# Two transformer blocks on one core: the SBUF addresses of the stage buffers moved, two of them with padded tiles

## The chip, the cores and the metric

The kernel runs on one core of one Trainium2 chip. The metric is the device time of one execution in microseconds (us); three executions give a median, and one more was profiled. The result must equal the reference's output for 256 tokens of width 1024 in float32.

## What is computed

Two blocks in sequence, over one batch of 256 tokens. The first is a SwiGLU FFN, a mixer of three attention branches, and a second SwiGLU FFN, with layer norms. The second is a mixer of a gated delta rule and a sparse attention, a GEGLU FFN with a convolution, and a gated embedding. Cut to what the change touches:

```
def swiglu(x, w_gate, w_up, w_down):
    return (jax.nn.silu(x @ w_gate) * (x @ w_up)) @ w_down          # D=1024, D_FF=2816
...
    x = layer_norm(alpha * x + 0.5 * swiglu(x, ...), ...)            # FFN 0
    x = layer_norm(alpha * x + hybrid_mixer(x, ...), ...)            # o_m, o_d, o_s -> branches -> w_out
    x = layer_norm(alpha * x + 0.5 * swiglu(x, ...), ...)            # FFN 1
...
    mixed = (g_a * (ya @ w_a2d[i]) + g_b * (yb @ w_b2d[i])) @ w_o[i]
    h = h + rmsnorm(mixed, norm_mix_post[i])
    f = rmsnorm(h, norm_ffn_pre[i]) @ w_up[i]
    f = causal_dwconv(f, conv_ffn[i]) + conv_ffn_b[i]
    f_gate, f_val = jnp.split(f, 2, axis=-1)
    f = (jax.nn.gelu(f_gate) * f_val) @ w_down[i]                    # FFN 2
```

## The kernel before

Every float32 product is made of three matmuls in a rounded type (fp32r): a value is split into a high part and a low part, and `mm3` (L585) adds high·high, the cross product and low·high in PSUM. Of every operand of such a product there are therefore two buffers, made by `pair` (`weights_high` and `weights_low`, `xT_high` and `xT_low`, and so on).

All weights come as one stream of 343 full chunks of 512 KB. SP loads a chunk into one of four slots of `ring`, ScalarE rounds it into `weights_high` (L1449), GpSimd subtracts to get `weights_low` (L536), and TensorE waits for that (`weights`, L563). A chunk is 8 blocks of 128x128. The semaphores `used`, `hi_ready` and `lo_ready` pass the slots round.

TensorE runs its program in one written order. A matmul has a stationary operand, loaded by a weight load (LDWEIGHTS, the row PEld of the profile) that runs beside the matmul before it, and a moving operand. Two forms occur:

- Feature-major: the stationary operand is a weight block of 128x128 and the moving one an activation tile of 256 columns. Of this form are the FFNs' gate and up, most projections, the branches (moving operand `oT`) and the delta rule's and sparse attention's output projections (`mix_part`, L1384, moving operand `yT`).
- Token-major: the stationary operand is 128 columns of an activation tile and the moving one up to 512 columns of weights. Of this form are the FFNs' down projections (`down`, stationary `hT`), the projections `w_out` and `w_o` (stationary `mT`), and some projections with `xT` as the stationary operand.

An FFN has 22 tiles of hidden features. After the first few, each step is one `gate_up` (48 matmuls of 256 columns) and one `down` (12 matmuls of 512 columns). VectorE makes the hidden tile `hf` and splits it into `hT_high` and `hT_low` (`split_hidden`, L2006), four tiles deep (GROUP). The delta rule's and attention's outputs are turned by TensorE, then split by ScalarE (`high_y`, L1858) and VectorE (`low_y`, L2594) into `yT`.

SBUF is laid out by the order of declarations in `build`. The tensors that live throughout come first: `ring`, `weights_high` and `weights_low` all begin at 128 modulo 1024 bytes of their partition (a block at 128 or 640), and `xT_high` and `xT_low` at 64, with tiles of 1024 bytes. After a filler of 144 words, `fill_stage`, comes one region that the stages use in turn: the FFNs (`hT`, `hf`, `act_buf`, `gel`), block one (`qkT`, `mT1`, `v1`, `oT` and others) and block two (`cv`, `mT2`, `yT`, `pE` and others). In the kernel before, this region begins at 32 modulo 1024 bytes, and so do all tiles of `hT`, `mT`, `oT` and `yT`, since each tile is 1024 bytes long.

Of the kernel before, what the change touches and what calls it, by code (L numbers as in the profile page):

```python
# [25 lines left out]
ALU = mybir.AluOpType  # L26
ACT = mybir.ActivationFunctionType
AX = mybir.AxisListType
F32 = mybir.dt.float32
F32R = mybir.dt.float32r  # L30

P = 128
T = 256
# [7 lines left out]
GROUP = 4  # L41
# [267 lines left out]
def build(nc, x_tm, x_fm, p_fm, stream, consts, cols, big_rows, small_rows, out, const_at):  # L309
# [4 lines left out]
    with ExitStack() as ctx:  # L314
        in_ffn, block_one, block_two, early = ExitStack(), ExitStack(), ExitStack(), ExitStack()

        def sb(name, shape, where=ctx, dtype=F32):
            return where.enter_context(nc.sbuf_tensor(name, [P] + list(shape), dtype))

        def pair(name, shape, where=ctx):  # L320

            return sb(name + "_high", shape, where, F32R), sb(name + "_low", shape, where, F32R)

        S = {n: ctx.enter_context(nc.semaphore(n)) for n in SEMS}
        arrived = [ctx.enter_context(nc.semaphore(f"arrived{i}")) for i in range(RING)]
        acc = ctx.enter_context(nc.psum_tensor("acc", [P, 4, 512], F32))
# [16 lines left out]
        nmx2 = sb("nmx2", [2, 4])  # L343
        den2 = sb("den2", [2, 4])
        coef2 = sb("coef2", [2, 4])
        sb("fill_stage", [144])
        hT = pair("hT", [GROUP, T], in_ffn)
        hf = sb("hf", [2, T], in_ffn)
        act_buf = sb("act_buf", [2, 2 * T], in_ffn)
        gel = sb("gel", [2, T], in_ffn)  # L350
# [43 lines left out]
        dec = sb("dec", [8, P], early)  # L394
        kv_tm = sb("kv_tm", [4, 512], early)
        early.close()
        yT = pair("yT", [8, T], block_two)
        sb("pad3", [3 * 8 * P + 4 * 512 - 16 * T], block_two)
        rcs = sb("rcs", [2, 16, 64], early, F32R)
        early.close()  # L400
        both_pT = sb("both_pT", [2, 2, 384], early)
# [156 lines left out]
        def _(pe):  # L558
# [4 lines left out]
            def weights(n):  # L563

                b = at[0]
                at[0] += n
                if b % CB == 0:
                    ch = b // CB
                    pe.wait_ge(S["lo_ready"], ch + 1)
                    release[0] = ch > 0  # L570
                return parts(b, n)
# [13 lines left out]
            def mm3(o, lhsT, rhs, start, stop, **kw):  # L585

                mm(o, lhsT[0], rhs[0], start, False, **kw)
                mm(o, lhsT[0], rhs[1], False, False, **kw)
                return mm(o, lhsT[1], rhs[0], False, stop, **kw)

            def cut(both, *at_):
                return tuple(x[(slice(None),) + at_] for x in both)
# [467 lines left out]
            for first in range(0, H1 + 4, 2):  # L1060
                for i in sb_heads(first):
                    o = take(f"sbz{i}")
                    r = 64 * (i % 2)
                    q, k = qkT[r:r + 64, 12 + i // 2, :], qkT[r:r + 64, 15 + i // 2, :]
# [4 lines left out]
                for h in sb_heads(first - 2):  # L1069
                    o = take(f"sbr{h}")  # L1070
# [10 lines left out]
                for h in sb_heads(first - 4):  # L1081
                    o = take(f"sbo{h}")
# [54 lines left out]
            for t in range(4):  # L1137
                o = take(f"l2_{t}")
# [71 lines left out]
            o = take("gcum")  # L1210
            pe.wait_ge(S["g_ready"], 1)
            for ch in range(2):
                last = nc.tensor.matmul(o[:, HG * ch:HG * ch + HG], c("upper"), gk[:, HG * ch:HG * ch + HG], start=True, stop=True)
            done(last)
            for ch in range(2):
                o = take(f"grow{ch}")
                pe.wait_ge(S["g_rows"], 1)
                for h in range(HG):
                    last = nc.tensor.matmul(o[:, h * P:(h + 1) * P], grow[:, HG * ch + h, :], c("upper"), start=True, stop=True)
# [3 lines left out]
            for ch in range(2):  # L1223
                assert jobs[now[0]][0] == f"brow{ch}"
                now[0] += 1
                for h in range(HG):
                    last = nc.tensor.matmul(acc[:, 2 + ch, h * P:(h + 1) * P], brep[:, HG * ch + h, :], ident, start=True, stop=True)
# [3 lines left out]
            for ch in range(2):  # L1231
                t0 = P * ch
                for name, first in ((f"ktm{ch}", 4), (f"vtm{ch}", 8)):
                    o = take(name)
                    for h in range(HG):
                        last = nc.tensor.transpose(o[:, h * P:(h + 1) * P], cv[:, first + h, t0:t0 + P], ident)
                    done(last)
                for name, first in ((f"kk{ch}", 4), (f"qk2_{ch}", 0)):
                    o = take(name)
# [139 lines left out]
            def mix_part(o, b):  # L1379

                for k in range(4):
                    if b == 0 and k % 2 == 0:
                        pe.wait_ge(S["yT_ready"], k // 2 + 1)
                    last = mm3(o[:, b * T:b * T + T], weights(1), cut(yT, 4 * b + k), k == 0, k == 3)  # L1384
                return last

            o = [bank(f"mix{n}") for n in range(3)]
# [16 lines left out]
            for n in range(3, 8):  # L1404
                o = take(f"mix{n}")
# [5 lines left out]
            for half in range(2):  # L1411
                w = [weights(4) for k in range(2)]
                for tok in range(2):
                    o = take(f"ple{2 * half + tok}")
# [12 lines left out]
        def _(act):  # L1427
# [430 lines left out]
            def high_y(k, order):  # L1858

                act.wait_ge(S["yT_turned"], order + 1)  # L1860
                nc.scalar.copy(yT[0][:, 2 * k:2 * k + 2, :].rearrange("p a t -> p (a t)"), acc[:, (k + 2) % 4, :]
                               ).then_inc(S["yT_high"], 1)

            def both_exp(e):
# [116 lines left out]
        def _(dve):  # L1981
# [24 lines left out]
            def split_hidden(n, f, it):  # L2006
                value = NF * n + f + 1 + GROUP * it
                dve.wait_ge(S["h_made"], value)
                v.tensor_copy(hT[0][:, f % GROUP, :], hf[:, f % 2, :]).then_inc(S["h_high"], 1)
                dve.wait_ge(S["h_high"], value)  # L2010
                v.tensor_tensor(hT[1][:, f % GROUP, :], hf[:, f % 2, :], hT[0][:, f % GROUP, :].bitcast(F32), ALU.subtract  # L2011
                                ).then_inc(S["hidden"], 1)

            def conv_col(i, it):
# [186 lines left out]
            def low(out, value, high):  # L2201

                return v.tensor_tensor(out, value, high.bitcast(F32), ALU.subtract)  # L2203
# [390 lines left out]
            def low_y(k, order):  # L2594

                dve.wait_ge(S["yT_high"], order + 1)
                hi, lo = (x[:, 2 * k:2 * k + 2, :].rearrange("p a t -> p (a t)") for x in yT)
                low(lo, acc[:, (k + 2) % 4, :], hi).then_inc(S["yT_ready"], 1)

            def both_bias(e):  # L2600

# [229 lines left out]
```

## Time and profile before

| | us |
|---|---|
| median of 3 runs | 1124.36 |
| lowest and highest | 1123.49, 1124.64 |
| the profiled execution | 1123.59 |
| its span, first to last instruction | 1121.8 |

| engine | busy us | share of the span | instructions |
|---|---|---|---|
| TensorE matmuls (PE) | 1094.6 | 98% | 8110 |
| TensorE weight loads (PEld) | 1023.9 | 91% | 8110 |
| GpSimd (POOL) | 902.6 | 80% | 695 |
| ScalarE (ACT) | 621.2 | 55% | 1002 |
| VectorE (DVE) | 498.7 | 44% | 904 |

Matmuls overlap: a matmul of 256 columns is shown as some 280 ns long, while the next one starts after some 115 ns. So the busy time of PE tells whether TensorE had work, not how fast it did it. How fast is read from the starts: the time from the first start to the last, divided by the number of matmuls between them, is called the interval below. The length that the profile shows for a matmul moves with it, by about as many ns.

### The profile page before, as it was taken

The numbers are of one execution on the slowest core, as the hardware profiler recorded it, in microseconds if no ns is written. First come the engines' busy times: TensorE is split into PE (matmuls) and PEld (weight loads), VectorE is DVE, ScalarE is ACT, GpSimd is POOL, SyncE is SP. The second block draws the span as 40 slices with busy tenths as digits, with TensorE's granted clock in tenths as the row PEclk, the third lists the DMA queues.
The fourth block names the chain that finished last, engine by engine and source line by source line (L and its number), as shares of the span: only waits on it lengthen the run. The fifth ranks groups of instructions, "written<-read, shape, count | busy, mean of one in ns | idle before, by whom it ended". The sixth has DMA issues, their size and how long they took to land.

```text
span 1121.8 us, 22284 instructions
## 1 busy us (share of the span) xinstructions
PE 1094.6 (98%) x8110; PEld 1023.9 (91%) x8110; DVE 498.7 (44%) x904; ACT 621.2 (55%) x1002; POOL 902.6 (80%) x695
## 2 busy tenths in 40 slices
PE   8999999999999999999999999999999999999997
PEld 7999998999998998999999899889999798999985
DVE  4422113202456554421126655774766256445563
ACT  4444444654667866544443775555666565555564
POOL 6999997897664596999999589577355898999985
PEclk9999999999999999999999999999999999999999
DMA  7866665676442364766665466335234565666662
GB/s 254 275 205 194 190 194 158 206 229 185 117 129 80 128 186 144 227 203 198 188 184 178 140 190 191 114 116 161 63 95 129 181 195 168 191 197 187 189 182 79
DMA packets 52774, 191.29 MB, mean 171 GB/s; under 512 B 5856, under 2 KB 6112, under 8 KB 52320
## 3 DMA queue, kind: packets, MB, share of 16 engines
q1 hardware_dynamic: 50688, 182.47, 53.1%
q10 hardware_dynamic: 2016, 7.81, 2.0%
q8 instruction: 53, 0.87, 0.3%
q14 instruction: 17, 0.14, 0.0%
HBM read 189.21 MB, written 1.05 MB: 170 GB/s over the span
## 4 chain that ended last, share of the span: by engine, by line
POOL 54%; issue 29%; PE 14%; POOLq 1%; ACT 1%; DMA 0%; DVE 0%; SPq 0%; DVEq 0%; ACTq 0%
POOL weights_low L536 54%; PE banks L578 8%; PE acc L578 6%; DMA ring<-in_stream 0%; POOLq L542 0%; POOLq L533 0%; ACT tmp L1697 0%; ACT tmp L1967 0%; ACT weights_high L1449 0%; DVE res L2173 0%; POOL stat L550 0%; DVE xs L2185 0%; POOLq L314 0%; PE banks L687 0%; SPq L497 0%
## 5 line engine op out<-in xcount | busy, mean ns | idle before, releaser
L536 POOL TENSOR_TENSOR weights_low<-ring,weights_high 128x512 fp32r<-128x512 f32 x686 | 899.5, 1344 | 207.6 <-ACT weights_high L1449 205.4
L1449 ACT CAST weights_high<-ring 128x1024 fp32r<-128x1024 f32 x343 | 356.0, 1047 | 215.7 <-PE banks L578 133.5
L578 PE MATMUL banks<-xT_high,weights_high 128*128 128x256 f32 x1264 | 351.6, 278 | 1.1 <-POOL weights_low L536 1.1
L578 PE MATMUL banks<-xT_low,weights_high 128*128 128x256 f32 x1264 | 350.5, 277 | 0.0
L578 PE MATMUL banks<-xT_high,weights_low 128*128 128x256 f32 x1264 | 350.4, 277 | 0.0
L578 PEld LDWEIGHTS banks<-xT_high,weights_high 128*128 128x128 f32 x1264 | 237.6, 188 | 4.1 <-issue 1.5
L578 PEld LDWEIGHTS banks<-xT_low,weights_high 128*128 128x128 f32 x1264 | 237.6, 188 | 2.3
L578 PEld LDWEIGHTS banks<-xT_high,weights_low 128*128 128x128 f32 x1264 | 237.9, 188 | 0.0
L2002 DVE TENSOR_TENSOR hf<-act_buf,banks 128x256 f32<-128x256 f32 x40 | 16.8, 421 | 225.7 <-ACT act_buf L1475 211.5
L578 PE MATMUL acc<-xT_high,weights_high 128*128 128x256 f32 x408 | 109.2, 287 | 1.9 <-ACT xT_high L1550 1.0
L578 PE MATMUL acc<-xT_high,weights_low 128*128 128x256 f32 x408 | 105.2, 278 | 0.0
L578 PE MATMUL acc<-weights_high,hT_high 128*128 128x512 f32 x264 | 104.1, 394 | 1.0 <-POOL weights_low L536 1.0
L578 PE MATMUL acc<-weights_low,hT_high 128*128 128x512 f32 x264 | 104.0, 394 | 0.0
L578 PE MATMUL acc<-weights_high,hT_low 128*128 128x512 f32 x264 | 103.3, 397 | 0.0
L578 PE MATMUL acc<-xT_low,weights_high 128*128 128x256 f32 x408 | 93.7, 278 | 0.6 <-DVE xT_low L2203 0.6
L578 PEld LDWEIGHTS acc<-xT_high,weights_high 128*128 128x128 f32 x408 | 75.2, 188 | 6.3 <-ACT xT_high L1550 1.7
L578 PEld LDWEIGHTS acc<-xT_high,weights_low 128*128 128x128 f32 x408 | 75.1, 188 | 0.0
L578 PEld LDWEIGHTS acc<-xT_low,weights_high 128*128 128x128 f32 x408 | 67.9, 188 | 0.8 <-DVE xT_low L2203 0.8
L2011 DVE TENSOR_TENSOR hT_low<-hf,hT_high 128x256 fp32r<-128x256 f32 x66 | 65.3, 990 | 2.3
L2027 DVE SCALAR_TENSOR_TENSOR act_buf<-banks,col,act_buf 128x255 f32<-128x255 f32 (+1 forms) x80 | 34.9, 478 | 58.7 <-ACT act_buf L1493 56.2
L578 PEld LDWEIGHTS acc<-weights_high,hT_low 128*128 128x128 f32 x264 | 49.6, 188 | 11.7
L578 PEld LDWEIGHTS acc<-weights_high,hT_high 128*128 128x128 f32 x264 | 49.6, 188 | 11.3 <-POOL weights_low L536 1.5
(362 smaller groups left out, 1579.4 us busy)
## 6 DMA issues: line engine op xcount, KB each, us to landing
ring<-in_stream SPq DMA_DIRECT2D x343, 512.0 KB, 3.7
rows<-in_big_rows ACTq DMA_DIRECT2D x3, 1024.0 KB, 7.6
rows<-in_big_rows ACTq DMA_DIRECT2D x3, 512.0 KB, 4.1
cst<-in_consts ACTq DMA_DIRECT2D x3, 470.5 KB, 6.5
xs<-in_x_tm ACTq DMA_DIRECT2D x2, 512.0 KB, 5.9
out<-xs SPq DMA_DIRECT2D x4, 256.0 KB, 2.1
gates<-in_x_fm SPq DMA_DIRECT2D x2, 256.0 KB, 4.1
ring<-in_stream SPq DMA_DIRECT2D x2, 256.0 KB, 4.1
```

The lines of the kernel that those rows point to most:

```text
L536: last = nc.gpsimd.tensor_tensor(wlo[:, slot, hs], ring[:, slot, hs], whi[:, slot, hs].bitcast(F32), ALU.subtract)
L578: ins = nc.tensor.matmul(o, lhsT, rhs, start=start, stop=stop, **kw)
L1449: nc.scalar.copy(whi[:, ch % RING, :], ring[:, ch % RING, :]).then_inc(S["hi_ready"], 1)
L2002: v.tensor_tensor(hf[:, f % 2, :], act_buf[:, f % 2, 0:T], ffn_tile(n, f, it)[:, T:2 * T], ALU.mult).then_inc(S["h_made"], 1)
L2011: v.tensor_tensor(hT[1][:, f % GROUP, :], hf[:, f % 2, :], hT[0][:, f % GROUP, :].bitcast(F32), ALU.subtract).then_inc(S["hidden"], 1)
L2027: last = v.scalar_tensor_tensor(buf, ffn_tile(2, f, it)[:, half * T:half * T + T - sh], conv_col(3 * (half * NF + f) + tap, it), buf, ALU. ...
```

## The change

The filler `fill_stage` grows from 144 to 152 words, so the region of the stages begins at 64 modulo 1024 bytes, 32 bytes later. The tiles of `hT` are declared 272 words long in place of 256 (1088 bytes apart) and those of `yT` 264 words long (1056 bytes apart); the 16 or 8 words behind the first 256 of each are never used. All instructions that touch `hT` and `yT` take the slice `0:T` of a tile, which turns two contiguous operands of `yT` (512 elements) into two runs of 256. A filler behind `yT` shrinks by as much.

| buffer | bytes modulo 1024 before | after |
|---|---|---|
| `weights_high`, `weights_low` (blocks) | 128, 640 | the same |
| `xT_high`, `xT_low` (all tiles) | 64 | the same |
| `hT_high`, tiles 0 to 3 | 32 each | 64, 128, 192, 256 |
| `hT_low`, tiles 0 to 3 | 32 each | 320, 384, 448, 512 |
| `yT_high`, tiles 0 to 7 | 32 each | 64, 96, 128 and so on to 288 |
| `yT_low`, tiles 0 to 7 | 32 each | 320, 352, 384 and so on to 544 |
| `mT1`, `mT2`, `oT`, `pE` (all tiles) | 32 | 64 |
| `hf`, `act_buf`, `gel` | 32 | 576 |

No instruction is added, removed or moved on any engine: the order of each engine's program is the same, and only these shapes differ (128x512 becomes 128x2x256 in the four casts at L1861 and the four subtractions of `low_y`).

```diff
@@ -343,8 +343,8 @@
-        sb("fill_stage", [144])
-        hT = pair("hT", [GROUP, T], in_ffn)
+        sb("fill_stage", [152])
+        hT = pair("hT", [GROUP, T + 16], in_ffn)
@@ -394,8 +394,8 @@
-        yT = pair("yT", [8, T], block_two)
-        sb("pad3", [3 * 8 * P + 4 * 512 - 16 * T], block_two)
+        yT = pair("yT", [8, T + 8], block_two)
+        sb("pad3", [3 * 8 * P + 4 * 512 - 16 * (T + 8)], block_two)
@@ -1381,7 +1381,7 @@
-                    last = mm3(o[:, b * T:b * T + T], weights(1), cut(yT, 4 * b + k), k == 0, k == 3)
+                    last = mm3(o[:, b * T:b * T + T], weights(1), cut(yT, 4 * b + k, slice(0, T)), k == 0, k == 3)
@@ -1858,7 +1858,7 @@
-                nc.scalar.copy(yT[0][:, 2 * k:2 * k + 2, :].rearrange("p a t -> p (a t)"), acc[:, (k + 2) % 4, :]
+                nc.scalar.copy(yT[0][:, 2 * k:2 * k + 2, 0:T], acc[:, (k + 2) % 4, :].rearrange("p (a t) -> p a t", a=2)
@@ -2006,9 +2006,9 @@
-                v.tensor_copy(hT[0][:, f % GROUP, :], hf[:, f % 2, :]).then_inc(S["h_high"], 1)
+                v.tensor_copy(hT[0][:, f % GROUP, 0:T], hf[:, f % 2, :]).then_inc(S["h_high"], 1)
...
-                v.tensor_tensor(hT[1][:, f % GROUP, :], hf[:, f % 2, :], hT[0][:, f % GROUP, :].bitcast(F32), ALU.subtract
+                v.tensor_tensor(hT[1][:, f % GROUP, 0:T], hf[:, f % 2, :], hT[0][:, f % GROUP, 0:T].bitcast(F32), ALU.subtract
@@ -2594,8 +2594,8 @@
-                hi, lo = (x[:, 2 * k:2 * k + 2, :].rearrange("p a t -> p (a t)") for x in yT)
-                low(lo, acc[:, (k + 2) % 4, :], hi).then_inc(S["yT_ready"], 1)
+                hi, lo = (x[:, 2 * k:2 * k + 2, 0:T] for x in yT)
+                low(lo, acc[:, (k + 2) % 4, :].rearrange("p (a t) -> p a t", a=2), hi).then_inc(S["yT_ready"], 1)
```

## Rows read from the trace of the kernel before

**Rows 1.** The page, part 1: busy us (share of the span), instructions; part 2, clock.
```profile
PE 1094.6 (98%) x8110; PEld 1023.9 (91%) x8110; DVE 498.7 (44%) x904; ACT 621.2 (55%) x1002; POOL 902.6 (80%) x695
PEclk9999999999999999999999999999999999999999
```

**Rows 2.** Waits of the engine PE: total us, times, longest.
```profile
PE banks L578 <- ACT gates L1623: 3.0, 3, 1.9
...
PE banks L578 <- POOL weights_low L536: 1.6, 2, 1.1
```

**Rows 3.** Busy time in the window of 17 FFN steps, then POOL's group there.
```profile
42.50:182.90 140.40, 140.40 (x1021) 131.16 (x1020) 28.01 (x51) 59.85 (x69) 134.03 (x105) 1.00 0.66 199
L536 POOL TENSOR_TENSOR weights_low<-ring,weights_high 128x512 fp32r<-128x512 f32 x105 | 135.5, 1320 | 6.4 <-ACT weights_high L1449 5.6
```

**Rows 4.** Timeline of PE, one FFN step: start us, us, engine, line, operation.
```profile
42.50 0.40 PE L578 MATMUL acc<-weights_high,hT_high 128*128 128x512 f32 x1
...
45.30 0.28 PE L578 MATMUL banks<-xT_high,weights_high 128*128 128x256 f32 x1
...
46.00 0.28 PE L578 MATMUL banks<-xT_high,weights_high 128*128 128x256 f32 x1
...
50.77 0.40 PE L578 MATMUL acc<-weights_high,hT_high 128*128 128x512 f32 x1
```

**Rows 5.** Timeline of PE, projection with `xT` as the stationary operand, 48 matmuls.
```profile
676.45 0.40 PE L578 MATMUL banks<-weights_high,xT_high 128*128 128x512 f32 x1
...
687.46 0.28 PE L578 MATMUL banks<-xT_high,weights_high 128*128 128x256 f32 x1
```

**Rows 6.** Timeline of PE, the branches (`oT`) and then `w_out` (`mT`).
```profile
398.53 0.28 PE L578 MATMUL banks<-oT_low,weights_high 128*128 128x256 f32 x1
...
412.14 0.40 PE L578 MATMUL acc<-weights_high,mT_high 128*128 128x512 f32 x1
...
434.55 0.38 PE L752 MATMUL banks<-cst 128*128 128x128 f32 x2
```

**Rows 7.** Timeline of PE, a stretch of `mix_part` (`yT`).
```profile
858.95 0.28 PE L578 MATMUL banks<-yT_high,weights_low 128*128 128x256 f32 x1
...
864.23 0.28 PE L578 MATMUL banks<-yT_high,weights_low 128*128 128x256 f32 x1
```

**Rows 8.** Timeline of PE, a fast stretch (projections qk), then a slow one (FFN 2).
```profile
204.25 0.28 PE L578 MATMUL acc<-xT_high,weights_high 128*128 128x256 f32 x1
...
239.39 0.33 PE L578 MATMUL banks<-weights_high,xT_high 128*128 128x384 f32 x1
...
904.09 0.28 PE L578 MATMUL acc<-xT_high,weights_high 128*128 128x256 f32 x1
...
931.88 0.39 PE L578 MATMUL acc<-weights_high,hT_high 128*128 128x512 f32 x1
```

**Rows 9.** Groups by shape in windows 645:667 and 687.6:706: busy us, mean ns.
```profile
L578 PE MATMUL banks<-xT_low,weights_high 128*128 128x256 f32 x62 | 17.4, 281 | 0.0
...
L578 PE MATMUL banks<-xT_low,weights_high 128*128 128x256 f32 x53 | 14.9, 281 | 0.0
```

**Rows 10.** Groups by shape in windows 37:183 (`hT`) and 676.5:687.3 (`xT` stationary).
```profile
L578 PE MATMUL acc<-weights_high,hT_low 128*128 128x512 f32 x69 | 27.4, 397 | 0.0
L578 PE MATMUL acc<-weights_low,hT_high 128*128 128x512 f32 x68 | 26.8, 394 | 0.0
L578 PE MATMUL acc<-weights_high,hT_high 128*128 128x512 f32 x68 | 26.7, 393 | 0.0
...
L578 PE MATMUL banks<-weights_low,xT_high 128*128 128x512 f32 x16 | 6.3, 394 | 0.0
L578 PE MATMUL banks<-weights_high,xT_high 128*128 128x512 f32 x16 | 6.3, 392 | 0.0
L578 PE MATMUL banks<-weights_high,xT_low 128*128 128x512 f32 x16 | 6.2, 389 | 0.0
```

**Rows 11.** What touches `yT`: duration ns min/median/max, first and last start.
```profile
L1861 ACT CAST yT_high<-acc x4: 562/586/593, 842.7 to 849.8; 128x512 fp32r<-128x512 f32 x4
L2203 DVE TENSOR_TENSOR yT_low<-acc,yT_high x4: 680/686/692, 843.6 to 850.6; 128x512 fp32r<-128x512 f32 x4
```

## The prediction

> **What bounds the kernel now.** I read the page first. TensorE has work for 98% of the span, and the clock granted to it is the higher of its two levels (2.4 GHz) throughout [rows 1]. The waits of TensorE come next: the longest kind is 3.0 us in all, and waits for GpSimd's `weights_low` at this line sum to 1.6 us [rows 2]. So nothing feeds TensorE late, and the end is set by how fast its 8110 matmuls follow each other. Idle time of the others is no cost, but it says how much faster TensorE may become before they limit it. In 17 FFN steps (140.40 us, 8.26 us each) GpSimd is idle for 6.4 us, 0.38 us a step [rows 3]. A saving below that goes to the end in full.
>
> An address can change three things only: how long an engine's own instruction takes, how long another's takes beside it, and so the interval from one matmul to the next. I therefore measured intervals in the timeline, with the addresses beside them.
>
> - FFN step [rows 4]: 12 matmuls of 512 columns with `hT` stationary (32 modulo 1024) from 42.50 to 45.30, 233 ns each; then 48 of 256 columns with `xT` moving (64) to 50.77, 114.0 ns each.
> - The same form with `xT` stationary (64) in place of `hT` (32), and the same moving weights: 676.45 to 687.46 for 48 matmuls, 229.4 ns [rows 5]. It is the nearest thing to the changed kernel that this trace holds.
> - `mT` stationary (32): 412.14 to 434.55 for 96, 233.4 ns [rows 6]. Like `hT`.
> - Moving operand at 32: `oT` 398.53 to 412.14 for 116, 117.3 ns [rows 6]; `yT` 858.95 to 864.23 for 45, 117.3 ns [rows 7].
> - Moving operand at 64 (`xT`): 310 matmuls from 204.25 to 239.39, 113.4 ns; but 236 from 904.09 to 931.88, 117.8 ns, with the same form and the same addresses modulo 1024 [rows 8].
>
> So there are two levels for a 256-column matmul, about 113.3 and 117.8 ns, and a long stretch keeps the one that it has. The length that the profile shows goes along: 281 ns in two more slow stretches of some 186 and 158 matmuls (in each, one of three groups of like size stands in the rows, x62 and x53) [rows 9]. At 64 both levels occur; at 32 I find the slow one alone. I infer that the read of the moving operand and the weight load beside it disturb each other, by an amount that depends on both addresses and on how one started against the other.
>
> **The change, part by part.** It adds no instruction, wait or transfer. The terms are sizes of intervals.
>
> 1. `hT` stationary, 3 FFNs x 22 tiles x 12 = 792 matmuls, now 233 ns. If its tiles behave as `xT` does, 229.4: 4 ns less, 792 x 4 = 3.2 us. This is the weak step: only tile 0 of `hT_high` comes to lie as `xT` lies; the others go to 128 up to 576 with 1088 bytes between them, and no row shows those. Bounds by the lengths shown [rows 10]: `hT`'s three kinds of matmul last 397, 394 and 393 ns, 394.7 in the mean; the shortest kind of this form is 389, the longest 397. If all of `hT`'s went to the one or the other, each would be 5.7 ns shorter or 2.3 longer. So between 4.5 us less and 1.8 us more. I take 229.4, since it is an interval and the addresses there are the nearest to the new ones.
> 2. `mT` stationary, 2 x 96 = 192 matmuls, at 233.4 now, and after the change exactly as `xT` is: 192 x 4 = 0.8 us less. Bounds as in term 1: 1.1 less and 0.4 more.
> 3. `oT` moving, 216 matmuls, after the change exactly as `xT`: 113.3 or 117.8 against 117.3, so 0.9 us less or 0.1 more. I take 0.5 less.
> 4. `yT` moving, 8 x 8 x 3 = 192 matmuls. Tile k lies 32k bytes further on against the weight blocks, which no row shows. 0.8 us less if all fall to 113.3; I take 0.4 less, and 0.8 more as the other bound.
> 5. The two runs of 256 in place of one of 512: four casts of 586 ns and four subtractions of 686 ns [rows 11]. The elements are the same. Nearest for a bound is nothing against one start more each; TensorE waits for these only around 843 to 851 us, so even 0.1 us each would show as 0.2 us. I take nothing.
> 6. Elsewhere (attention, delta rule) buffers move by 32 bytes too. The engines that use them wait on chains that are hidden or short; taken as nothing, with 1 us to either side.
>
> Sum: 3.2 + 0.8 + 0.5 + 0.4 = 4.9 us less. In an FFN step the saving is 0.05 us, far below GpSimd's 0.38 us of slack [rows 3], so it is not taken back. The profiled execution's 1123.59 becomes 1118.7; against the median of 1124.36 it is 1119.5.
>
> The trace's 233 against 229.4 ns for the same moving operand [rows 4, 5] says that the place of the stationary tile matters. The Trainium skill ("TensorE: Matmul & The Clock Gate", Part 2, Step-by-step) says otherwise: TensorE has two independent SBUF read ports, and loading the next tile's weights takes no read bandwidth from the running matmul. By that rule every term above would be nothing.
>
> **The rivals.**
>
> *A, nothing happens.* The 4 ns of rows 4 and 5 would then come from something else than the address: the order of units, or PSUM. For it: a 256-column stretch has two levels at one address [rows 8], so the address alone doesn't decide. Against: `hT` and `mT`, in different orders, both show 233, and `oT` and `yT` both 117.3. The time would be 1124.4, within 2.2 us. The rule of the Trainium skill just named is this rival; so is what the Trainium skill says in "SBUF — State Buffer" (Who interferes with whom), that PE never waits on anyone.
>
> *B, the fast level is lost in the FFN.* After each `down`, `gate_up` starts slowly: six intervals from 45.30 to 46.00, 117 ns each; then it finds the fast level, since all 48 average 114.0 [rows 4]. What it starts from is the rhythm that the `hT` matmuls leave behind. If the new rhythm lets it stay on the slow level, as FFN 2's first stretch does [rows 8], about 43 matmuls in each of the 53 `gate_up` that follow a `down` cost 4.5 ns more: 10.3 us. With the other terms kept, 1119.5 + 10.3 = 1129.8, slower. It decides from half of the steps on (5.1 us more against 4.9 less). For it: the slow level is stable once held; against it: the 17 steps of rows 3 take 8.26 us each, just as the one of rows 4 (42.50 to 50.77), so all 17 leave it now.
>
> *C, the slow stretches turn fast.* By the intervals, some 1230 matmuls on `xT` lie in slow stretches, among them those of rows 8 and 9. 1230 x 4.5 ns = 5.5 us. If the changed start of each such stretch frees most, 1119.5 - 5.5 = 1114.0. For it: such a stretch follows code whose operands move by 32 bytes. Against: half of them follow a wait, whose end no address sets.
>
> *D, the change doesn't do what it says.* The declared sizes give the addresses, and the order of instructions is the same; I give it no chance of its own.
>
> **How the numbers follow.** Forecast (some us less, no level flips at large): 0.40. A: 0.18. B: 0.22. C: 0.20. The predicted time is the forecast's, 1119.5. The range runs from C's 1114.0, a little lower for the bounds of terms 1 and 2, to 1113.0; upward it goes past A's 1126.6 into B, to 1128.5. That leaves out the far part of B and a corner of C, less than 2 in 10. What a measurement can tell from no change is about 0.2%, 2.2 us. Faster: forecast and C, 0.60. Same: 0.18. Slower: 0.22.
>
> **What would show it.** In the changed kernel's timeline, a `down` should last 2.75 us in place of 2.80, and a whole FFN step 8.21 in place of 8.26; the `w_out` matmuls 229.4 ns each; those of `oT` 113 or 118. The lengths shown for `hT` matmuls (0.39 and 0.40) should fall by some 4 ns in the mean. I am wrong in step 1 if `down` stays at 2.80 or rises; by B if `gate_up`'s 48 matmuls need more than 5.6 us in place of 5.47; by C if the stretches of 281 ns are shown at 276. The waits for `weights_low` should stay near 1.6 us: if they grow by as much as intervals shrink, GpSimd has become the bound and the slack was misread.

## The result, and the profile after

The changed kernel takes 1127.51 us (median of 7 runs, 1127.14 to 1128.33) against 1124.36 us (7 runs beside it, 1123.21 to 1125.59). The ratio is 1.0029, with a 95% interval of 1.0019 to 1.0038: slower by 0.3%, 3.2 us. The profiled execution took 1127.53 us, with a span of 1125.7 against 1121.8.

The page of the changed kernel, parts 1 and 2, as in [rows 1]:

```profile
PE 1099.4 (98%) x8110; PEld 1031.6 (92%) x8110; DVE 487.9 (43%) x904; ACT 621.3 (55%) x1002; POOL 901.8 (80%) x695
...
PEclk9999999999999999999999999999999999999998
```

Its waits of the engine PE (waiter, who it waited for: us in total, times, longest), as in [rows 2]:

```profile
PE banks L578 <- ACT gates L1623: 2.0, 1, 2.0
PE acc L578 <- POOL weights_low L536: 1.8, 5, 0.5
PE banks L1140 <- DVE rows L2450: 1.7, 2, 1.1
PE banks L578 <- POOL weights_low L536: 1.5, 2, 1.0
```

The same view of the kernel before has one more line for `weights_low` than [rows 2] show:

```profile
PE acc L578 <- POOL weights_low L536: 1.0, 3, 0.5
```

The counts of instructions are as before, ACT and POOL are within 0.8 us of theirs, and DVE has 10.8 us less. The waits for `weights_low` at `banks` are 1.5 us (1.6 before), those at `acc` 1.8 us (1.0 before). The clock is as before but for one stretch of 3.4 us. The window 362:365, first in the kernel before, then in the changed one (us, busy time of PE, PEld, DVE, ACT, POOL, then the granted clock, DMA share and GB/s):

```profile
362.00:365.00 3.00, 3.00 (x25) 2.89 (x24) 2.86 (x5) 1.97 (x4) 2.56 (x3) 1.00 0.40 82
362.00:365.00 3.00, 3.00 (x16) 2.64 (x15) 2.38 (x5) 2.99 (x5) 2.54 (x3) 0.50 0.00 0
```

From 361.8 to 365.3 us the changed kernel's TensorE was granted 0.50, the lower level of 1.2 GHz, behind a wait of 1.97 us; the kernel before waits 1.88 us at the same place and kept 1.00. Against the kernel before the 20 intervals there are 1.6 us longer. No run shows that the addresses have to do with it: of the other profiles of full kernels below, the filler alone, the padded tiles alone and the run in which `hT` stays have one such stretch each, the run with tiles 1280 bytes apart has two, and the remaining three have none.

PE's busy time rose, by 4.8 us. Most of it lies inside the FFN steps. The timeline of PE in the changed kernel, four steps in a row: each pair of rows is the start of a `down` and the start of the `gate_up` behind it (compare [rows 4]).

```profile
59.25 0.40 PE L578 MATMUL acc<-weights_high,hT_high 128*128 128x512 f32 x1
...
62.02 0.28 PE L578 MATMUL banks<-xT_high,weights_high 128*128 128x256 f32 x1
...
67.67 0.39 PE L578 MATMUL acc<-weights_high,hT_high 128*128 128x512 f32 x1
...
70.39 0.28 PE L578 MATMUL banks<-xT_high,weights_high 128*128 128x256 f32 x1
...
76.05 0.39 PE L578 MATMUL acc<-weights_high,hT_high 128*128 128x512 f32 x1
...
78.84 0.28 PE L578 MATMUL banks<-xT_high,weights_high 128*128 128x256 f32 x1
...
84.30 0.39 PE L578 MATMUL acc<-weights_high,hT_high 128*128 128x512 f32 x1
...
87.07 0.28 PE L578 MATMUL banks<-xT_high,weights_high 128*128 128x256 f32 x1
...
92.72 0.40 PE L578 MATMUL acc<-weights_high,hT_high 128*128 128x512 f32 x1
```

The differences of these starts, with the tile of `hT` that the `down` reads:

| tile of `hT` | place modulo 256, high and low | `down`, us | `gate_up` behind it, us |
|---|---|---|---|
| 0 | 64, 64 | 2.77 | 5.65 |
| 1 | 128, 128 | 2.72 | 5.66 |
| 2 | 192, 192 | 2.79 | 5.46 |
| 3 | 0, 0 | 2.77 | 5.65 |
| before, all tiles | 32, 32 | 2.80 | 5.47 |

Each `down` is as long as before or shorter, and the `gate_up` behind three of four has gone from 114.0 ns a matmul to 117.8, the slow level of [rows 8]. This repeats with period four through all three FFNs: 38 of the 53 `gate_up` that follow a `down` are slow, none before. (Why the table counts modulo 256 is what the experiments show.)

The lengths in the same window as [rows 10], by shape (mean ns is the last number before the second bar), say the same: `hT`'s matmuls 392 to 393 in place of 393 to 397, `xT`'s 280 in place of 277.

```profile
L578 PE MATMUL banks<-xT_low,weights_high 128*128 128x256 f32 x283 | 79.2, 280 | 0.0
...
L578 PE MATMUL acc<-weights_high,hT_low 128*128 128x512 f32 x69 | 27.1, 392 | 0.0
L578 PE MATMUL acc<-weights_low,hT_high 128*128 128x512 f32 x68 | 26.7, 393 | 0.0
```

The program is the same 8110 matmuls in the same order, so each interval can be set against its own of before. Summed by kind, in us, after less before:

| matmuls | all intervals | without those that hold a wait |
|---|---|---|
| `gate_up` behind a `down` (2544) | +6.8 | +6.7 |
| on `hT` (792) | -2.0 | -2.1 |
| on `oT` (216) | -0.6 | -0.9 |
| on `mT` (192) | -0.5 | -0.9 |
| on `yT` (192) | 0.0 | +0.2 |
| on `xT` elsewhere (2807) | -1.2 | -0.5 |
| the rest (1366) | +1.5 | -0.1 |
| sum | +3.9 | |

Two parts of the 3.9 us are not the addresses' as far as any run shows. The first 12 matmuls, part of the rest, take 1.1 us more: matmuls at the very start follow each other every 427 ns and later every 216, and the shorter distance comes behind the 8th matmul before and behind the 14th after. The stretch at the lower clock holds 0.9 us of the row `xT` elsewhere, which would stand at -2.1 without it, and 0.7 us of the rest. These two parts differ from one profile to the next, so that what the change costs is read from the medians (3.2 us), and where it arises from the rows.

### The profile page after: what moved, and what is told of

The parts are those of the page before. It is cut to its first block, busy times and chain, and to the rows that moved or that the text cites. A ratio compares the mean times of both kernels' runs of the same rounds, so it can differ in the third digit from the quotient of the medians.

```text
span 1125.7 us, 22284 instructions
## 1 busy us (share of the span) xinstructions
PE 1099.4 (98%) x8110; PEld 1031.6 (92%) x8110; DVE 487.9 (43%) x904; ACT 621.3 (55%) x1002; POOL 901.8 (80%) x695
## 4 chain that ended last, share of the span: by engine, by line
POOL 55%; issue 28%; PE 14%; POOLq 1%; ACT 1%; DMA 0%; DVE 0%; SPq 0%; DVEq 0%; ACTq 0%
POOL weights_low L536 55%; PE banks L578 8%; PE acc L578 6%; DMA ring<-in_stream 0%; POOLq L542 0%; POOLq L533 0%; ACT tmp L1697 0%; ACT tmp L1967 0%; ACT weights_high L1449 0%; DVE res L2173 0%; POOL stat L550 0%; DVE xs L2185 0%; POOLq L314 0%; PE banks L687 0%; SPq L497 0%
## 5 line engine op out<-in xcount | busy, mean ns | idle before, releaser
L2011 DVE TENSOR_TENSOR hT_low<-hf,hT_high 128x256 fp32r<-128x256 f32 x66 | 59.8, 907 | 2.3
```

The source lines that it names most:

```text
L2011: v.tensor_tensor(hT[1][:, f % GROUP, 0:T], hf[:, f % 2, :], hT[0][:, f % GROUP, 0:T].bitcast(F32), ALU.subtract).then_inc(S["hidden"], 1)
```

## The experiments

Two theories stood after this. Theory one: TensorE's read of the moving operand and the weight load beside it disturb each other by their places, and the rhythm in which a `down` ends picks the level of the `gate_up` behind it. Theory two: the padded distance, the start at 64, or other engines' accesses are harmful in themselves.

### The filler alone

```diff
-        sb("fill_stage", [144])
+        sb("fill_stage", [152])
```

> Only the filler grows (144 to 152 words); hT and yT keep tiles of 1024 bytes. The changed kernel loses 3 of 4 gate_up to the slow level (5.65 us in place of 5.47), and its down takes 2.80, 2.775, 2.767 and 2.72 us by tile. Theory (the rhythm in which down ends sets the level, and the distance of 1088 makes it differ by tile): all tiles now lie at 64 modulo 1024, so all steps are alike: down 2.75 us (229.4 ns each, as the projection with xT stationary), and gate_up on one level in all steps. If the distance of 1088 was the harm, gate_up is fast everywhere, a step takes 8.21 us and the time is about 1119.5 us. Rival (the start at 64 itself was the harm): gate_up is slow in all steps, 5.65 us, and the time about 1131 us. Rival (neither, chance of the run): a mix as in the changed kernel, about 1127.

Measured: 1124.21 us, ratio 0.9994 (0.9979 to 1.001). No difference in the median, but ten runs lie between 1120.10 and 1127.97, where the kernel before, beside it, lay between 1123.8 and 1126.9. The timeline of PE, one step of FFN 0, then one of FFN 2, in the same execution:

```profile
59.39 0.39 PE L578 MATMUL acc<-weights_high,hT_high 128*128 128x512 f32 x1
...
62.14 0.28 PE L578 MATMUL banks<-xT_high,weights_high 128*128 128x256 f32 x1
...
67.60 0.39 PE L578 MATMUL acc<-weights_high,hT_high 128*128 128x512 f32 x1
...
1052.34 0.40 PE L578 MATMUL acc<-weights_high,hT_high 128*128 128x512 f32 x1
...
1055.10 0.28 PE L578 MATMUL banks<-xT_high,weights_high 128*128 128x256 f32 x1
...
1060.76 0.40 PE L578 MATMUL acc<-weights_high,hT_high 128*128 128x512 f32 x1
```

FFN 0 and FFN 1 run 2.75 + 5.46 us a step. In FFN 2 the first `gate_up` is fast too, then comes a gap of 0.64 us before the next `down`, and the 16 steps behind it run 2.77 + 5.65, with the same addresses. So my expectation that all steps would be alike was wrong in one way: with `hT` at 64 the steps have two orbits (an orbit is a pair of lengths that repeats itself from step to step), and an FFN keeps the one that it has until something else comes between. One orbit costs 0.207 us more a step, 3.3 us over these 16 steps. A different number of slow FFNs from run to run would give the spread, but this isn't shown: I saw the orbits in one profile only, and that profile also holds a stretch at the lower clock (1.6 us).

### The padded tiles alone, start at 32

```diff
-        hT = pair("hT", [GROUP, T], in_ffn)
+        hT = pair("hT", [GROUP, T + 16], in_ffn)
...
-        yT = pair("yT", [8, T], block_two)
+        yT = pair("yT", [8, T + 8], block_two)
```

> The filler stays at 144 words, so the stage buffers begin at 32 modulo 1024; hT and yT have the padded tiles (1088 and 1056 bytes). mT and oT are as in the kernel before. Theory (rhythm by tile): the four tiles of hT lie at 32, 96, 160, 224 (high) and 288 to 480 (low), so the four steps differ; some gate_up are slow, each at 5.65 in place of 5.47 us, others fast. If half are slow, some 4.8 us more than before, less up to 2 us from faster down: about 1127. Rival (the start at 64 was the harm): like before, 1124, or a little less, with all gate_up fast.

Measured: 1130.95 us, ratio 1.0057 (1.004 to 1.0074). The slowest of the four combinations of start and distance: 39 of 53 `gate_up` are slow, and `down` takes 2.79 to 2.81 us, so nothing is earned. Its timeline:

```profile
51.73 0.39 PE L578 MATMUL acc<-weights_high,hT_high 128*128 128x512 f32 x1
...
60.18 0.39 PE L578 MATMUL acc<-weights_high,hT_high 128*128 128x512 f32 x1
...
68.43 0.39 PE L578 MATMUL acc<-weights_high,hT_high 128*128 128x512 f32 x1
...
76.89 0.40 PE L578 MATMUL acc<-weights_high,hT_high 128*128 128x512 f32 x1
```

Steps of 8.45, 8.25 and 8.46 us, against 8.27 before. The start at 64 is not the harm; the padded distance of `hT` is, from either start.

### TensorE alone: a map of the places

Each stretch is of this form (`at` picks the place):

```diff
+            for s in range(0, 1024, 32):       # 512 columns: stationary tile at s, moving weights at 128
+                reset()
+                for n in range(24):
+                    mm(acc[:, n % 4, :], hh(0, s, P), w(n % 2, 128, 512))
+            for m in range(0, 1024, 32):       # 256 columns: moving tile at m, stationary blocks at 128 and 640
+                reset()
+                for n in range(24):
+                    mm(banks[:, n % 2, 0:T], w(n % 3 == 2, 128 + 512 * (n // 3 % 2), P), xx(n % 3 == 1, m, T))
```

> No part of the reference's work: TensorE alone, 32 stretches of 24 matmuls of 512 columns with the moving weights at 128 modulo 1024 bytes and the stationary tile at 0, 32 up to 992; then 32 stretches of 24 matmuls of 256 columns with the stationary blocks at 128 and 640 and the moving tile at 0 to 992. No other engine works and no transfer runs beside it. Theory (moving read and weight load disturb each other by their relative place): in the first part the interval depends on the stationary tile's place, from 226.7 ns (as the third and quickest down of the changed kernel, tile at 128) over 229.4 (at 64) to 233.3 (at 32); in the second it is 113.3 or 117.8 ns at 64 and another at 32. Rival (other engines' reads and writes of SBUF make the difference): all stretches alike, since the others are silent.

Measured: all 32 places of each part fall into 8 classes, by the place modulo 256. The map and the three runs with TensorE alone that follow are one execution each. Two stretches in the timeline of PE, second matmul and last, with the stationary tile at 64 and then at 128:

```profile
50.44 0.40 PE L66 MATMUL acc<-w_low,h_high 128*128 128x512 f32 x1
...
55.48 0.39 PE L66 MATMUL acc<-w_low,h_high 128*128 128x512 f32 x1
...
63.32 0.40 PE L66 MATMUL acc<-w_low,h_high 128*128 128x512 f32 x1
...
68.31 0.40 PE L66 MATMUL acc<-w_low,h_high 128*128 128x512 f32 x1
```

22 intervals in each: 5.04 us or 229 ns, and 4.99 us or 227 ns. The table gives the mean of the last 17 intervals of each stretch; the four stretches of a class agree within 0.1 ns, except where a range stands.

| place modulo 256 of the tile that is varied | 0 | 32 | 64 | 96 | 128 | 160 | 192 | 224 |
|---|---|---|---|---|---|---|---|---|
| 512 columns, stationary tile varied, ns | 232.2-232.9 | 233.4 | 228.9 | 233.4 | 226.7 | 233.5 | 233.5 | 234.3 |
| 256 columns, moving tile varied, ns | 118.8-119.1 | 117.2-118.6 | 113.4 | 118.5 | 119.7 | 116.9 | 117.8 | 119.8 |

No other engine touches SBUF here, and the numbers are those of the kernels: `hT` at 32 233 ns, `xT` stationary at 64 229, `xT` moving at 64 113.3. The rival of other engines' accesses is out for these values. The four tiles of the changed kernel lie in the classes 64, 128, 192 and 0; 12 times the table gives 2.75, 2.72, 2.80 and 2.79 us, near their 2.77, 2.72, 2.79 and 2.77. (The 512-column part varies the stationary tile alone, with the moving weights at 128.)

### TensorE alone: the FFN step with `hT` at 25 places

```diff
+            for h, l, m in COMBOS:
+                for n in range(2):
+                    down(h, l)
+                    gate_up(n, m)
```

> No part of the reference's work: TensorE alone repeats the FFN step (down of 12 matmuls, gate_up of 48) twice for each of 25 places of hT_high and hT_low, with xT at 64 and the weights at 128 modulo 1024. Theory: with hT at 32 and 32 it repeats the step of the kernel before (down 2.80, gate_up 5.47 us, fast level reached); with the four places of the changed kernel its four steps: 64 and 320 down 2.767 and slow 5.65, 128 and 384 down 2.72 and slow, 192 and 448 down 2.80 and fast 5.45, 256 and 512 down 2.775 and slow. Some place is fast in both and would make a step of 8.17 us. Rival (history or other engines decide): the level doesn't go with the place.

Measured, second step of each place: 32 and 32 gives 2.797 + 5.466 us, as the kernel before. 128 gives 2.720 + 5.655, 96 and 224 are slow too (5.65 to 5.66). Place 64 was slow when the step before was (2.766 + 5.655), and fast when it was fast (2.747 + 5.466): the two orbits of the filler's run. Place 160 was slow in its first step and fast in its second, all three times. Places 0 and 192 turn the level over: at 0, entered from a slow step, the first step was fast and the second slow in all four cases (5.44 to 5.45, then 5.65); at 192 the first was fast and the second slow when entered from a slow step, and the other way round in the two cases entered from a fast one.

So half of what I expected held: the place matters, and at some places the level before matters as well. That is also the pattern of the changed kernel, where the four places take turns: 64 and 128 stay slow, 192 turns to fast, 0 turns back to slow. The step of 8.17 us that I hoped for exists at no place; the shortest here is 8.21.

### TensorE alone: is it the distance?

```diff
+            for s in range(0, 256, 32):        # stationary blocks at s, moving tile at m, two ways to start
+                for m in range(0, 256, 32):
+                    for start in range(2):
+                        reset()
+                        if start:
+                            mm(acc[:, 3, :], hh(0, 128, P), w(0, 128, 512))
+                            mm(acc[:, 3, :], hh(0, 128, P), w(0, 128, 512))
```

> No part of the reference's work: TensorE alone, 256 columns, the stationary blocks at s and s+512, the moving tile at m (s and m each 0, 32 up to 224, modulo 256), 20 matmuls each, once after float32 matmuls and once after two matmuls of 512 columns. Theory (only the distance of the two places modulo 256 counts, and how the stretch starts): the interval is the same along s - m; 113.3 ns where s - m is 64, as in the first map at 128 and 64, and there 113.3 or 117.8 by the start. Rival (the places themselves count): the values at one distance differ.

Measured (mean of the last 13 intervals of a stretch), over the eight pairs and two starts at each distance:

| s - m modulo 256 | 0 | 32 | 64 | 96 | 128 | 160 | 192 | 224 |
|---|---|---|---|---|---|---|---|---|
| ns | 119.5-120.0 | 118.0-118.5 | 113.3 or 117.8 | 117.3-120.0 | 118.4-120.2 | 119.7-120.4 | 113.3 or 117.8 | 116.4-117.8 |

At a given distance the eight pairs of places agree: within 0.5 ns at 0 and 32, and where they differ by more (up to 2.7 ns, at 96), the two starts of one pair differ by as much (120.0 and 117.5 at s = 160, m = 64). So the distance counts, not the places, as far as 256 columns go. Two distances have two levels, with nothing between them: at 64 a stretch was fast in 10 cases of 16 (7 of 8 after the float32 matmuls, 3 of 8 after the 512-column ones), at 192 in 5 of 16. `xT` against the weight blocks is at a distance of 64 (128 less 64), `oT` and `yT` of before at 96. The start of a stretch picks the level.

### TensorE alone: which `down` leaves `gate_up` fast from either side

```diff
+            for h, l in COMBOS:
+                for first in (32, 128):
+                    down(first, first)
+                    gate_up(1, 64)
+                    for n in range(2):
+                        down(h, l)
+                        gate_up(n, 64)
```

> No part of the reference's work: TensorE alone. For hT_high at 64 and 128 modulo 256 and hT_low at each of 0 to 224, two FFN steps after a step that leaves gate_up on the fast level (hT at 32), and two after one that leaves it slow (hT at 128). Theory (the level of gate_up is set by the rhythm of the down before it, and that by both places and by the level before): with 64 and 64 both orbits hold, 2.747 + 5.466 after a fast step, 2.767 + 5.653 after a slow one; with 128 and 128 always slow. Some other place of hT_low ends down in another rhythm and leaves gate_up fast from either side, at a step of 8.2 us or less. Rival (the level goes by hT_high alone): all eight of 128 slow.

Measured, `down` + `gate_up` in us, second step:

| `hT_high`, `hT_low` modulo 256 | after a fast step | after a slow step |
|---|---|---|
| 64, 64 | 2.748 + 5.466 | 2.767 + 5.653 |
| 64, 160 | 2.748 + 5.465 | 2.747 + 5.470 |
| 64, 224 | 2.747 + 5.466 | 2.748 + 5.470 |
| 64, 192 | 2.797 + 5.449 | 2.797 + 5.454 |
| 128, 64 | 2.777 + 5.457 | 2.773 + 5.653 |
| 128, 128 | 2.720 + 5.654 | 2.720 + 5.654 |
| 128, 192 | 2.776 + 5.457 | 2.776 + 5.461 |

The timeline of PE after a slow step: the first `down` of 64 and 64, the `gate_up` behind it and the second `down`, then the same three of 64 and 160:

```profile
168.40 0.40 PE L67 MATMUL acc<-w_high,h_high 128*128 128x512 f32 x1
...
171.16 0.28 PE L67 MATMUL banks<-x_high,w_high 128*128 128x256 f32 x1
...
176.82 0.40 PE L67 MATMUL acc<-w_high,h_high 128*128 128x512 f32 x1
...
317.54 0.40 PE L67 MATMUL acc<-w_high,h_high 128*128 128x512 f32 x1
...
320.31 0.28 PE L67 MATMUL banks<-x_high,w_high 128*128 128x256 f32 x1
...
325.78 0.39 PE L67 MATMUL acc<-w_high,h_high 128*128 128x512 f32 x1
```

From the same slow level, 64 and 64 goes on at 5.66 us (171.16 to 176.82) and 64 and 160 goes over to 5.47 (320.31 to 325.78). The level doesn't go by `hT_high` alone: of the eight pairs with 128, three (`hT_low` at 32, 192 and 224) are fast from either side. The pair 64 and 160 shares with 64 and 224 the shortest step among those without a second orbit, 8.21 us.

### `hT` stays, the other stage buffers move

```diff
         in_ffn.close()
+        sb("shift", [8])
```

> hT, hf, act_buf and gel stay as in the kernel before (32 modulo 1024, 1024 bytes apart); all buffers of block one and block two begin at 64, with tiles of 1024 bytes. Theory (the loss of the changed kernel is in the FFN steps alone): FFN steps as before, 2.80 + 5.47 us; mT 228.9 ns in place of 233.4, 0.4 us less in each of the two projections; oT 0.7 to 0.9 less; yT between 0.8 less and nothing: about 1122.3. Rival (the stage buffers' start also moves the levels of the xT stretches between): 1124 or more, with more slow xT matmuls outside the FFN steps.

Measured: 1123.85 us, ratio 1.0002 (0.9993 to 1.0011). The FFN steps were as before, but I had expected 2 us less and got nothing that can be measured. In its profile `mT` took 233.3 ns in `w_out` and 232.4 in `w_o`, at the very places where it took 228.9 and 229.1 in the changed kernel, and `oT` earned 0.2 us in place of 0.9. So `mT` at 64 has more than one level as well: the profiles below with `mT` at 64 and `yT` at 64 show 229.1 in `w_out` and 232.4 in `w_o`. I take it that what the block buffers earn at 64 is a matter of how their stretches start; no run tests that by itself. The rival's premise held in part: outside the FFN steps the `xT` stretches did change, to the fast side (1.9 us less without the intervals that hold a wait), which in this profile the stretch at the lower clock hides.

### Two versions made from the map

The first puts the pair 64 and 160 into the kernel before, with the filler of 152 words:

```diff
-        sb("fill_stage", [144])
-        hT = pair("hT", [GROUP, T], in_ffn)
+        sb("fill_stage", [152])
+        hT_first = sb("hT_high", [GROUP, T], in_ffn, F32R)
+        sb("fill_hT", [24], in_ffn)
+        hT = hT_first, sb("hT_low", [GROUP, T], in_ffn, F32R)
```

> Stage buffers begin at 64 modulo 1024, tiles of 1024 bytes, and hT_low lies 96 bytes further on: hT_high at 64, hT_low at 160 modulo 256. By the runs with TensorE alone this pair ends every down so that gate_up is fast, from either level before: down 2.747, gate_up 5.466 us in all three FFNs and in every run. 53 steps x (8.267 - 8.213) = 2.9 us less, 0.5 us less in oT and up to 0.8 in mT: about 1120.5, and the runs lie within 1 us or so, unlike those of the filler alone (1120.1 to 1128.0). Rival (the level is a matter of chance once hT is off 32): some FFN is slow in some runs, 3.7 us each.

Measured: 1120.76 us, ratio 0.9972 (0.9962 to 0.9983), and eight runs within 1.8 us (1120.07 to 1121.87), not quite the 1 us expected, where the filler alone had spread over 7.9 and the kernel before, beside it, over 2.2. (`hf`, `act_buf` and `gel` lie 96 bytes further on too; with TensorE alone only `hT_low` moved.) All steps of all three FFNs are alike, but for the first `gate_up` of FFN 2, which a gap of 0.4 to 0.6 us follows in every profile; one later step of FFN 2, where the filler alone had been slow:

```profile
1056.73 0.39 PE L580 MATMUL acc<-weights_high,hT_high 128*128 128x512 f32 x1
...
1059.47 0.28 PE L580 MATMUL banks<-xT_high,weights_high 128*128 128x256 f32 x1
...
1064.94 0.39 PE L580 MATMUL acc<-weights_high,hT_high 128*128 128x512 f32 x1
```

The second also moves `mT1` and `mT2` to 128 modulo 256, the moving weights' own place:

```diff
+        sb("pad0", [16], block_one)
         mT1 = pair("mT1", [KD, T], block_one)
-        sb("pad1", [18 * T - 2 * KD * T], block_one)
+        sb("pad1", [18 * T - 2 * KD * T - 16], block_one)
...
+        sb("pad2", [16], block_two)
         mT2 = pair("mT2", [KD, T], block_two)
...
+        sb("pad_y", [48], block_two)
         yT = pair("yT", [8, T], block_two)
-        sb("pad3", [3 * 8 * P + 4 * 512 - 16 * T], block_two)
+        sb("pad3", [3 * 8 * P + 4 * 512 - 16 * T - 48], block_two)
```

> As the run before, and mT1 and mT2 lie at 128 modulo 256, the place of the moving weights, where the map shows 226.7 ns. 192 matmuls at 226.7 in place of 233.4 or 228.9: 0.4 to 1.3 us less than the run before, about 1119.6. Rival: mT stays at 233, since its units come in another order.

Measured: 1119.99 us, ratio 0.9965 (0.9951 to 0.9978), the lowest median here, though its interval overlaps with the one of the run before. `w_o` takes 227.1 ns a matmul. `w_out` runs from 411.29 to 433.07, 96 matmuls of 226.9 ns (233.4 in [rows 6]):

```profile
411.29 0.39 PE L583 MATMUL acc<-weights_high,mT_high 128*128 128x512 f32 x1
...
433.07 1.27 PE L757 MATMUL banks<-cst 128*128 128x128 f32 x10
```

### The shortest `down`, on purpose

```diff
+        sb("fill_hT", [16], in_ffn)
         hT = pair("hT", [GROUP, T], in_ffn)
```

> As the filler alone, but hT_high and hT_low both at 128 modulo 256: each down alone is at its quickest, 2.72 us, and by the runs with TensorE alone every gate_up after it is slow, 5.655: a step of 8.375 in place of 8.267. 53 x 0.108 = 5.7 us more than before, less 0.9 for oT and mT: about 1129, slower than the changed kernel, although its down is 0.055 us shorter. Rival (the level of gate_up doesn't come from the place of hT): gate_up fast, 1118.

Measured: 1128.79 us, ratio 1.0035 (1.0023 to 1.0048), as expected: the shortest `down` of all, and only the padded tiles alone were slower. All 53 `gate_up` are slow:

```profile
60.29 0.39 PE L579 MATMUL acc<-weights_high,hT_high 128*128 128x512 f32 x1
...
63.01 0.28 PE L579 MATMUL banks<-xT_high,weights_high 128*128 128x256 f32 x1
...
68.66 0.39 PE L579 MATMUL acc<-weights_high,hT_high 128*128 128x512 f32 x1
```

### The changed kernel with another padded distance

```diff
-        hT = pair("hT", [GROUP, T + 16], in_ffn)
+        hT_first = sb("hT_high", [GROUP, T + 64], in_ffn, F32R)
+        sb("fill_hT", [24], in_ffn)
+        hT = hT_first, sb("hT_low", [GROUP, T + 64], in_ffn, F32R)
```

> The changed kernel with the tiles of hT 1280 bytes apart in place of 1088 and hT_low 96 bytes further on, so that modulo 256 all tiles of hT_high lie at 64 and all of hT_low at 160; yT keeps its 1056. Theory (only the place modulo 256 counts, not the distance of the tiles as such): FFN steps of 2.748 + 5.466 us, all 53 gate_up fast, and the time of the run with that pair at a distance of 1024, 1120.8, plus up to 0.6 us for yT's padded tiles. Rival (a padded distance is harm in itself): some gate_up at 5.65, 1124 or more.

Measured: 1121.59 us, ratio 0.9973 (0.9965 to 0.9982). All steps of its profile take 8.21 us, but for the one with that gap. Its twelve runs spread over 4.1 us (1119.94 to 1124.07; the kernel before, beside it, over 3.9), so one orbit in the FFNs doesn't by itself make the times agree. A padded distance of `hT` does no harm here if it is a multiple of 256; 1088 is 64 over one, and so gives each of the four tiles another class. On `yT`, whose 1056 walks through all eight classes, the profiles with it show 0.1 to 0.2 us more than before, and those with tiles of 1024 bytes at 64 show 0.2 to 0.5 less. That is too little for the times.

## Why the prediction was wrong, step by step

- **The step that failed** is the choice between the forecast and rival B: "no level flips at large" had 0.40, B 0.22. B is what happened: 38 of 53 `gate_up` went to the slow level, which cost 6.8 us, and the mark named for it, `gate_up` over 5.6 us, is there (5.65). The argument against it, that all 17 steps leave the slow level now, was evidence about `hT` at 32 alone; it said nothing of the new places. That 1127.5 lies inside the range is due to its upper end, which reached into B; the forecast had the wrong sign.
- **B's price** per step was right, 43 x 4.5 ns = 0.19 us against 6.8 / 38 = 0.18 measured. It was too high in all, 10.3 us, as it took all 53 steps. B's 1129.8 less these 3.5 us, plus the 1.2 us that term 1 earned too little, gives the measured 1127.5; that it comes out so closely is luck, since other terms moved too.
- **The point from which B decides**, half of the steps, was about right: with the stretch at the lower clock left out, the gains of the second table are 5.2 us over all intervals (2.0 + 0.6 + 0.5 + 2.1) and 4.2 without those that hold a wait (2.1 + 0.9 + 0.9 + 0.5 - 0.2), which 24 to 29 steps at 0.18 us use up. 38 is beyond it.
- **What bounds the kernel** held: TensorE is busy for 98% of the span before and after, and in the FFN steps GpSimd still has slack (idle for 8.2 us in the 142 us of 17 steps, 6.4 before). But the prediction counted the waits for `weights_low` at `banks` alone, 1.6 us; with those at `acc` they are 2.6 us before and 3.3 after.
- **Two levels, and that a stretch keeps its own** held. The cause that I inferred, the two places against each other, is supported for 256 columns: the distance modulo 256 sets the interval, or the two levels it can have, with all other engines silent. For 512 columns only the stationary tile was moved. That it is the weight load's read that gets in the way was not tested, since no matmul here runs without a load.
- **Term 1** was mis-sized: `hT` earned 2.0 us, not 3.2. I took all tiles to behave as the one row at 64. By classes they stand at 228.9, 226.7, 233.5 and 232.3.
- **Terms 2 and 3** came out at 0.5 to 0.9 us each, about as forecast, but partly by luck: the runs in which `hT` stays and with `hT` at 64 and 160 have `mT` and `oT` at the same places and got less from them. **Term 4** was 0.4 less forecast and 0.0 to 0.2 more measured. **Term 5** at nothing held: in the median the four casts took 582 ns (586 before) and the four subtractions 685 (686 before). **Term 6** wasn't measured apart: the `xT` stretches elsewhere earned 2.1 us with the stretch at the lower clock left out, more than the 1 us given to either side.
- **Rival A** is out. The Trainium skill ("TensorE: Matmul & The Clock Gate", Part 2, Step-by-step) says that TensorE has two independent SBUF read ports and that loading the next tile's weights takes no read bandwidth from the running matmul. If that made the place of the stationary tile free, the map would be flat; it shows 226.7 to 234.3 ns for the same moving operand. The measurement decides: the place isn't free, whatever the ports do.
- **Rival C** did not happen: the `xT` stretches outside these `gate_up` earned 2.1 us at most, not 5.5.

## What to carry to other kernels

Where matmuls bound the time, measure the interval between starts, not busy time, and look at each operand's place modulo 256 against that of the operand beside it; up to 4.5% of a stretch hung on 32 bytes here (113.4 against 118.5 ns in the map). A place that makes one kind of matmul quick can leave the next kind on a slow level, so the unit to measure is the whole repeating step, entered from both levels, and a place that comes out fast from either is worth more than one that comes out fast from one. Tiles that take turns, as the four of `hT` do, should lie a multiple of 256 bytes apart, or each has a rhythm of its own. And before two profiles are set against each other, look at the granted clock of each: a stretch of 3.4 us at the lower level, 1.6 us of time, came and went here, and no run tells why.

## What the runs showed of the hardware that I had not expected

- The interval of fp32r matmuls depends on addresses modulo 256 bytes: at 256 columns on the distance of moving and stationary operand, 113.3 to 120.4 ns; at 512 columns, with the moving operand at 128, on the place of the stationary one, 226.7 to 234.3 ns.
- At distances of 64 and 192, 256-column matmuls have two stable levels, 113.3 and 117.8 ns, with the same operands; the matmuls just before pick one, and a stretch keeps it: 310 matmuls at 113.4 and 236 at 117.8 ns in [rows 8].
- A loop of two kinds of matmul can so have two orbits, 8.21 and 8.42 us a step, in one execution of one program; with TensorE alone, changing only the place of `hT_low` by 96 bytes took the second away. In the kernel all 53 steps then ran at the shorter one, but for the one that holds a wait, and the times spread over 1.8 us (8 runs) in place of 7.9 (10 runs); with the same places and tiles 1280 bytes apart over 4.1 (12 runs).
- At some places (0 and 192) the step turned the level over each time, so a ring of tiles at different places repeats a fixed pattern of slow and fast steps.
